# A two-layer GLA/FoX trunk with grouped experts: the residual stays in SBUF through the expert loop, and the router's logits are taken from uncentred rows

## The reference

```python
h = layer_norm(ALPHA * h + mix, ln_g[layer, 0], ln_b[layer, 0])
ffn = grouped_moe(h, router_w, router_bias, moe_w_gate[layer], moe_w_up[layer], moe_w_down[layer])
h = layer_norm(ALPHA * h + ffn, ln_g[layer, 1], ln_b[layer, 1])
# grouped_moe
scores = softmax(xt @ router_w)          # then the best group of 4 experts, and its best 2
h = silu(xt @ w_gate[e]) * (xt @ w_up[e]) * gate[e]
y = sum over the 2 chosen experts of h @ w_down[e]
```

## Time and profile before

| | |
|---|---|
| median of 3 runs | 1231.17 us |
| the profiled execution's own time | 1230.52 us |
| its span | 1228.8 us |
| TensorE busy | 1193.8 us (97%) |
| VectorE busy | 893.2 us (73%) |
| ScalarE busy | 703.7 us (57%) |
| GpSimd busy | 183.9 us (15%) |
| DMA, mean | 229 GB/s |
| weight loads of the experts, each | 1 MB, 12 to 13 us from issue to landing |

### The profile page before, as it was taken

One profiled execution on the slowest core, in us unless ns is written; L12 is line 12 of the kernel. 1 busy time (PEld: TensorE's weight loads), 2 busy tenths in 40 slices (PEclk: granted clock), 3 DMA queues, 4 the chain that ended last, 5 costly groups with the idle time before them and its releaser, 6 DMA issues.

```text
span 1228.8 us, 14990 instructions
## 1 busy us (share of the span) xinstructions
PE 1193.8 (97%) x5802; PEld 945.0 (77%) x5803; DVE 893.2 (73%) x1159; ACT 703.7 (57%) x866; POOL 183.9 (15%) x158
## 2 busy tenths in 40 slices
PE   7999999999999999999999999999999999999995
PEld 5787588877888888876887766768878888888873
DVE  5275555678999998989433555675679999998886
ACT  4432523357687786774333554573267778777672
POOL 1000100211132221210000000000212222122111
PEclk9999999999999999999899999999999999999998
DMA  8223021179999999987111420322289999999973
GB/s 286 71 85 122 1 103 70 52 257 411 358 368 378 368 370 377 358 340 281 69 70 52 154 86 18 103 84 88 78 314 381 373 362 376 379 367 371 370 276 137
DMA packets 66346, 281.52 MB, mean 229 GB/s; under 512 B 12854, under 2 KB 13110, under 8 KB 41698
## 3 DMA queue, kind: packets, MB, share of 16 engines
q1 hardware_dynamic: 49248, 247.55, 53.2%
q0 software_dynamic: 12288, 28.42, 8.1%
q10 hardware_dynamic: 4738, 4.57, 1.1%
HBM read 270.99 MB, written 25.20 MB: 241 GB/s over the span
## 4 chain that ended last, share of the span: by engine, by line
PE 83%; DMA 7%; DVE 6%; issue 2%; ACT 1%; POOL 0%; DVEq 0%; SPq 0%; ACTq 0%; POOLq 0%
PE ps L717 22%; PE ps L719 22%; PE ps L718 22%; DMA ring<-in_moe_w_up_dram 4%; PE ps L885 2%; PE ps L1168 2%; PE ps L1178 2%; DVE ring_r L1613 2%; PE ps L1191 2%; DMA ring<-in_moe_w_down_dram 1%; PE ps L894 1%; DMA ring<-in_kv_w_dram 1%; PE ps L822 1%; PE ps L1099 1%; PE ps L1087 1%
## 5 line engine op out<-in xcount | busy, mean ns | idle before, releaser
L1613 DVE TENSOR_TENSOR ring_r<-ring,ring_r 128x2048 fp32r<-128x2048 f32 x128 | 291.7, 2284 | 7.8 <-ACT ring_r L1346 7.8
L1346 ACT CAST ring_r<-ring 128x2048 fp32r<-128x2048 f32 x128 | 242.6, 1927 | 15.7 <-DMA ring<-in_moe_w_gate_dram 9.8
L718 PE MATMUL ps<-ring_r,xgT_r 128*128 128x512 f32 x528 | 205.9, 390 | 0.0
L1346 ACT CAST high_r<-ring 128x2048 fp32r<-128x2048 f32 x64 | 122.2, 1913 | 113.4 <-DMA ring<-in_moe_w_up_dram 113.4
L1613 DVE TENSOR_TENSOR ring_r<-ring,high_r 128x2048 fp32r<-128x2048 f32 x64 | 146.1, 2289 | 36.3 <-ACT high_r L1346 35.9
L613 POOL DMA_INDIRECT sum_rows<-arena,tokv x28 | 57.7, 2062 | 389.6 <-ACT arena L1399 389.6
L718 PEld LDWEIGHTS ps<-ring_r,xgT_r 128*128 128x128 f32 x528 | 99.3, 188 | 18.8
L717 PE MATMUL ps<-ring_r,xgT_r 128*128 128x512 f32 x272 | 109.1, 401 | 0.2 <-DVE ring_r L1613 0.2
L719 PE MATMUL ps<-ring_r,xgT_r 128*128 128x512 f32 x272 | 106.1, 390 | 0.0
L717 PE MATMUL ps<-high_r,xgT_r 128*128 128x512 f32 x256 | 102.9, 402 | 1.2 <-DVE xgT_r L1827 1.1
L717 PE MATMUL ps<-featT,ring_r 128*128 128x512 f32 x256 | 103.8, 405 | 0.0
(11 more groups left out here) (288 smaller groups left out, 2118.8 us busy)
## 6 DMA issues: line engine op xcount, KB each, us to landing
ring<-in_moe_w_gate_dram SPq DMA_DIRECT2D x64, 1024.0 KB, 12.2
ring<-in_moe_w_up_dram SPq DMA_DIRECT2D x64, 1024.0 KB, 13.0
ring<-in_moe_w_down_dram SPq DMA_DIRECT2D x64, 1024.0 KB, 12.4
ring<-in_gla_w_in_dram SPq DMA_DIRECT2D x6, 2048.0 KB, 9.8
ring<-in_kv_w_dram SPq DMA_DIRECT2D x4, 2048.0 KB, 12.8
ring<-in_fox_w_qg_dram SPq DMA_DIRECT2D x4, 2048.0 KB, 8.1
ring<-in_gla_w_out_dram SPq DMA_DIRECT2D x2, 2048.0 KB, 7.8
h_rows<-arena POOLq DMA_DIRECT2D x8, 512.0 KB, 2.9
```

The source lines that it names most:

```text
L718: pe.matmul(o, left[0], right[1], start=False, stop=False)
L1346: act.copy(high, w).then_inc(half_high, 1)
L1613: dve.tensor_tensor(low, w, high.bitcast(F32), ALU.subtract).then_inc(half_low, 1)
```

## The change

1. The router's weights are multiplied by the gains ahead of time, one copy per layer. For this the gains are loaded as 16 rows of 128 by two small DMAs behind piece 5, TensorE turns them ahead of unit 12, and VectorE makes `g*W` and its column sums.
2. TensorE turns each half tile as soon as VectorE has taken it out of PSUM, in the middle of the next unit. The logits are made in halves too. VectorE's centring now waits until the rows have been turned. The mean times the column sums is subtracted from the logits.
3. The scaling of the last tile is cut in two strided halves, one ahead of the logits' arrival and one behind the difference that ScalarE's exponential waits for.
4. The residual stays in `H`. `sum_rows` becomes one DRAM tensor per layer, filled with zeros by two DMAs that ScalarE issues after unit 15. At the end of a loop the sums are loaded into another place (`moe_sums`), and GpSimd adds each tile to `H`.
5. Two waits are new: `load_sums` waits for the last up-projection, and GpSimd's second-norm work comes behind its four additions.

```diff
# SyncE
                     if n == 3:
                         sp.dma_start(shift_w, ...)
...
+                    if n == 5:
+                        for L in range(DEPTH):
+                            sp.dma_start(gain_rows[L * K:(L + 1) * K, :], ln_g[L, 0:1, :].rearrange("a (k p) -> (a k) p", p=P)
+                                         ).then_inc(shift_loaded, 16)
             def load_sums(L):
...
+                sp.wait_ge(half_used, half_count(L, half_of("up", E - 1, 1)))
                 for t in range(T):
-                    sp.dma_start(H[:, t, :], sum_rows[t * P:(t + 1) * P, :]).then_inc(sums_loaded[t], 16)
+                    sp.dma_start(moe_sums[:, t, :], sum_rows[L][t * P:(t + 1) * P, :]).then_inc(sums_loaded[t], 16)
# GpSimd, start and end of experts
+            const(pool.memset(zeros, 0.0))
...
+                pool.wait_ge(h_ready, T * (2 * L + 1))
+                for t in range(T):
+                    pool.wait_ge(sums_loaded[t], 16 * (L + 1))
+                    pool.tensor_tensor(H[:, t, :], H[:, t, :], moe_sums[:, t, :], ALU.add).then_inc(h_ready, 1)
# TensorE
+LOGITS_AFTER = ({m: (m - 1,) for m in range(1, 2 * T)}, {1: (0,), 3: (2, 1), 4: (3,), 5: (4,), 6: (5,), 7: (6,)})
+            def out_unit(L, u0, m):
+                unit(u0 + m, ks=range(K // 2))
+                if m:
+                    turn_rows_half(L, u0, m - 1)
+                unit(u0 + m, frees=2 if m == 2 * T - 1 else 0, ks=range(K // 2, K))
+                for n in LOGITS_AFTER[L].get(m, ()):
+                    logits_half(L, u0, n)
             def entry_end(L):
                 pe.wait_ge(half_high, half_count(L, 0))
                 idle_products(4, 7)
-                turn_centred(L, T - 1)
+                turn_rows_half(L, OUT_UNITS[L], 2 * T - 1)
                 idle_products(2, 7)
-                logits(L, T - 1)
+                logits_half(L, OUT_UNITS[L], 2 * T - 1)
+            def turn_rows_half(L, u0, m):
+                kk, t = units[u0 + m][2]
+                pe.wait_ge(*taken(u0 + m))
...
+                if m >= 2:
+                    pe.wait_ge(rows_taken, 2 * T * L + m - 1)
+                for j in range(4):
+                    mm = pe.transpose(ps[:, m % 2, j * P:(j + 1) * P],
+                                      H[:, t, (4 * kk + j) * P:(4 * kk + j + 1) * P], ident[:, :])
+                mm.then_inc(rows_turned, 1)
             for u in range(2 * H_A, U_GLA_TAIL):
+                if u == U_GLA_TAIL - 4:
+                    pe.wait_ge(shift_loaded, 16 * (2 * DEPTH + 1))
...
+                    pe.transpose(ps[:, 6, P:P + DEPTH * K], gain_rows, ident[0:DEPTH * K, 0:DEPTH * K]
+                                 ).then_inc(shift_done, 1)
# ScalarE
             take(U_GLA_TAIL - 1)
+            act.wait_ge(consts, 18)
+            for L in range(DEPTH):
+                act.dma_start(sum_rows[L].rearrange("(p r) (c n) -> p (r c) n", p=P, n=P),
+                              zeros.unsqueeze(1).to_broadcast([P, T * K, P])).then_inc(sums_clear, 16)
...
-                for t in range(T):
-                    act.wait_ge(h_scaled, T * L + t + 1)
-                    act.dma_start(sum_rows[t * P:(t + 1) * P, :], H[:, t, :]).then_inc(sums_begun, 16)
# VectorE, rows_normed and router
+                        dve.wait_ge(rows_turned, turned_halves(L, t))
                         dve.scalar_tensor_tensor(out=H[:, t, :], in0=H[:, t, :], scalar=ln_mv[:, t, 0:1], ...
-                scale(N, T - 1)
...
+                do(dve.tensor_tensor(rt[9], over_e(ln_mv[:, :, 0]), each_t(shift_logits[:, DEPTH + L, :], E), ALU.mult))
+                dve.wait_ge(rows_centred, T * L + T)
+                scale_last(2 * L, 0)
                 dve.wait_ge(rt_logits, L + 1)
-                do(dve.tensor_tensor(logits, ps[...], over_e(ln_r[:, :, 1]), ALU.mult))
+                do(dve.tensor_tensor(logits, ps[...], rt[9], ALU.subtract))
+                do(dve.tensor_tensor(logits, logits, over_e(ln_r[:, :, 1]), ALU.mult))
                 do(dve.tensor_tensor(logits, logits, each_t(shift_logits[:, L, :], E), ALU.add))
                 do(dve.tensor_reduce(rv[0], logits, AX.X, ALU.max))
                 dve.tensor_tensor(rt[0], logits, over_e(rv[0]), ALU.subtract).then_inc(rt_in, 1)
+                scale_last(2 * L, 1)
                 dve.wait_ge(rt_exp, L + 1)
# VectorE, second norm: add_first, add_sums
-                    dve.wait_ge(sums_loaded[t], 16 * (L + 1))
+                    dve.wait_ge(h_ready, T * (2 * L + 1) + t + 1)
```

More of the change, by code:

```diff
@@ L74, in yoco_trunk @@
     cum_rows = nc.dram_tensor("cum_rows", [16, S], F32).ap()
-    sum_rows = nc.dram_tensor("sum_rows", [S, D], F32).ap()
+    sum_rows = [nc.dram_tensor(f"sum_rows{L}", [S, D], F32).ap() for L in range(DEPTH)]
     RING, PAIRED = 6, 5
@@ L370, in yoco_trunk, with turned_halves @@
             plan("ob", fox0 + 8 + p, (p, t), "dve")
+        OUT_UNITS = (U_GLA_TAIL + 8, U_OUT)
+        LOGITS_AFTER = ({m: (m - 1,) for m in range(1, 2 * T)}, {1: (0,), 3: (2, 1), 4: (3,), 5: (4,), 6: (5,), 7: (6,)})
+        def turned_halves(L, t, kk=None):
+            at_m = [m for m in range(2 * T) if units[OUT_UNITS[L] + m][2][1] == t and kk in (None, units[OUT_UNITS[L] + m][2][0])]
+            return 2 * T * L + at_m[-1] + 1
         def unit_of(kind, blk):
@@ L609, in gather, with scatter @@
                                         bounds_check=last_row, oob_is_err=False).then_inc(done, 16)
-            def scatter(src, rows, done):
+            def scatter(L, src, rows, done):
                 pool.sem_inc(moves, 1)
-                pool.indirect_dma_start(out=sum_rows, out_offset=bass.IndirectOffsetOnAxis(ap=rows, axis=0),
+                pool.indirect_dma_start(out=sum_rows[L], out_offset=bass.IndirectOffsetOnAxis(ap=rows, axis=0),
                                         in_=src, in_offset=None, bounds_check=last_row, oob_is_err=False,
@@ L657, in experts @@
                                 pool.wait_ge(c_yd, c + 1)
[L658 removed]
+                                scatter(L, cyb, cold_rows[:, 1:2], c_sca)
                             pool.wait_ge(c_sca, (before + 3) * 16)
@@ L783, in tail @@
                         transpose_tile(TP_MIX[L], s - 1, src)
[L785 to L793 removed]
+                for m in range(2 * T):
+                    if m % 2 == 0:
+                        pe.wait_ge(tp_dve, 2 * (4 * TP_MIX[L] + m // 2 + 1))
+                    out_unit(L, u0 + 8, m)
+                entry_end(L)
+            def out_unit(L, u0, m):
[5 more added lines that the diff above has]
+                    logits_half(L, u0, n)
             def idle_products(n, bank):
@@ L1113, in _ @@
                     pe.wait_ge(z_abs, T)
-                    pe.matmul(ps[:, 6, 0:DEPTH * E], one[:, :].to_broadcast([P, P]),
+                    pe.matmul(ps[:, 6, 0:2 * DEPTH * E], one[:, :].to_broadcast([P, P]),
                               shift_sum.rearrange("p a e -> p (a e)"), start=True, stop=True).then_inc(shift_done, 1)
@@ L1209, in _ @@
             for m in range(8):
-                unit(U_OUT + m, frees=2 if m == 7 else 0)
-                if m in (3, 4, 6):
-                    turn_centred(1, (3, 4, 6).index(m))
-                if m in (5, 6, 7):
-                    logits(1, m - 5)
+                out_unit(1, U_OUT, m)
             entry_end(1)
@@ L1290, in take_normed @@
             def take_normed(L):
-                for t in range(T):
-                    for kk in range(2):
-                        act.wait_ge(centred_turned, 2 * (T * L + t) + kk + 1)
-                        act.copy(turned[:, 4 * kk:4 * kk + 4, t * P:(t + 1) * P],
-                                 ps[:, kk, :].rearrange("p (k n) -> p k n", k=4)).then_inc(centred_taken, 1)
-                    if t < T - 1:
-                        scale_residual(L, t)
+                for m in range(2 * T):
+                    kk, t = units[OUT_UNITS[L] + m][2]
+                    act.wait_ge(rows_turned, 2 * T * L + m + 1)
+                    act.copy(turned[:, 4 * kk:4 * kk + 4, t * P:(t + 1) * P],
+                             ps[:, m % 2, :].rearrange("p (k n) -> p k n", k=4)).then_inc(rows_taken, 1)
+                    if L == 0 and kk == 0 and t:
+                        scale_residual(L, t - 1)
+                    if L == 1 and m in (3, 4, 6):
+                        scale_residual(L, (3, 4, 6).index(m))
             def scale_residual(L, t):
                 act.wait_ge(ln_ready, 2 * L * T + t + 1)
-                act.mul(dealt(H[:, t, :], K), blocks(Hp[:, t, :], K), ALPHA).then_inc(h_scaled, 1)
+                act.mul(dealt(H[:, t, :], K), blocks(Hp[:, t, :], K), ALPHA).then_inc(h_ready, 1)
             def tail(L):
@@ L1667, in rows_normed, with scale_last @@
                         done.append(t)
-                dve.wait_ge(rows_centred, T * L + T)
-                scale(N, T - 1)
+            def scale_last(N, part):
+                c, t = slice(part * P // 2, (part + 1) * P // 2), T - 1
```

(10 more changed lines are left out.)

85 lines of the change are left out of this document (39 added, 46 removed).

## The result

The changed kernel takes 1280.26 us (median of 4 runs, 1277.98 to 1280.32), beside 1232.49 us for the kernel before in the same comparison: ratio 1.0377, 95% interval 1.0336 to 1.0418. The forecast was 1252 us, range 1238 to 1267. The sign was right and the size was not: +48 us and not +21. The profiled execution has a span of 1276.2 us beside 1228.8, so there are 47.4 us to find.

The account below looks back on a forecast made before the run. The prediction took TensorE (97% busy) to bound the kernel, with DMA also full in the expert loops. Its terms summed to +21.1 us on the profiled 1230.5 us, plus 0.65 us to the median: 1252 us, range 1238 to 1267.

Parts of the forecast that it names:

- gains: Ahead of unit 12: TensorE waits for the gains' load behind piece 5, +7.7 us, and +1.5 us for its clock.
- zeros: At the heads: issuing the fills holds ScalarE, so TensorE's third output waits, +9.7 us, and +1.0 us for the clock.
- out stages: Both out stages: more half turns and half logits before the last unit ends, 2.1 us each, +4.2 us in all.
- the fifth block: Second layer's out stage: VectorE takes this block late and TensorE wants it in the next unit, +0.5 us.
- the chain behind them: From the last unit's end to the operation behind the exponential: 7.7 us against 7.8 before, counted as 0.
- loops: Expert loops: without storing the residual, TensorE gets back 2 us of idle time per layer, -4.0 us in all.
- GpSimd's additions: Layer ends: four additions of 1.9 us each may delay GpSimd's first norm step; +0.5 us first layer, 0 second.
- Rival B: Expert loops: DMA bounds them and the saved traffic returns in full, 2 x 5.7 us; 1228.4 us, chance 0.06.
- Rivals A and C: A: ScalarE not held by the fills, 1241.6 us, chance 0.22; C: slower fills, clock down through heads, 1267.5 us, chance 0.12.

Follow-up runs that it names:

- the router part alone: Kernel before with logits from uncentred rows, gains loaded behind piece 3 and 29 idle products, residual still through DRAM: 1240.2 us (ratio 1.0069).
- the two kernels of the residual part: Kernel before with the residual kept in SBUF and zero fills by SyncE: 1235.58 us with additions by VectorE, 1228.65 us with additions by DMA.
- the kernel with early gains: Changed kernel with the gains loaded behind piece 3 and not behind piece 5: 1270.5 us (ratio 1.0301).

## Why the prediction came out too low

From the marks, the terms measured against the forecast are (us): gains 10.4 (9.2 with the clock), zeros 7.4 (10.7), out stages 5.5 (4.7 with the fifth block), the chain behind them -0.5 (0), picked experts to gates 8.1 (0), gates to the first hidden blocks 0.8 (0), loops -1.8 (-4.0), last hidden block to first sum 15.4 (0.5), first norm to out stage 2 2.2 (0). Of the 26 us that were missing, 15 are the additions and 8 the tables, both put at about nothing.

- **Gains, +7.7 and +1.5 for the clock: right.** 8.34 us of standstill (8.4 forecast) and about 2.3 us of half clock (twelve matmuls at 0.2 us more each); undone, 9.8 us.
- **Zeros, +9.7 and +1.0: that the issue holds ScalarE is right, the rule for its end is not, and the size was too large.** ScalarE was held 12.5 us and not 17.2. The prediction had it held until only 2500 pieces were open; 4968 packets had still not begun. The prices were good: a piece of 512 B took 27.2 ns (30 forecast) and piece 6 stood in the way for 6.3 us per DMA engine (6.5 forecast), by the row below. Only 3256 packets of the fills came first, 5.5 us per engine and not 10.7. Undone, 9.2 us; between the changed kernel's marks 7.4 us (17.72 at the end of the heads less 10.35 at unit 15).

DMA queues of the changed kernel from 110 to 136.61 us, where the issue ended (packets, MB, share of 16 engines; q1 is SyncE's with piece 6, q10 ScalarE's with the fills):

```profile
q1 hardware_dynamic: 1040, 2.10, 23.7%
q10 hardware_dynamic: 3256, 1.67, 20.8%
```

- **Out stages, +4.2: nearly right**, 2.7 and 2.8 us and not 2.1 each. The +0.5 us for the fifth block shows only as the 0.1 between the two.
- **"The logits come early, but VectorE isn't free for them ... I count 0": the chain right, the conclusion wrong.** From the last eviction to the operation behind the exponential it is 7.5 us (7.7 forecast). But TensorE's 20 idle products begin with the early logits. They ended 2.0 us before the picked experts came, the clock fell, and the tables took 3.7 and 4.4 us more. With 29 idle products this went. The step that failed is asking only whether VectorE gains by early logits, and not what TensorE does in the time. The later second half of the scaling, some 2 us at the gather, lay hidden under it.
- **GpSimd's additions, +0.5 and 0: the step that failed most.** I sized them by their own length (1.9 us forecast, at most 2.8; 2.3 us beside the one-hots and 3.3 beside the splits) and asked who waits for them. Nobody waited for them; VectorE's work beside them was kept out. It cost 5.9 us in the first layer, and in the second 9.4 us with the clock. The prediction took it, without a word, that GpSimd and VectorE work side by side at no cost to each other; with that fall both the +0.5 and "in the second layer ... I count nothing". That the second layer pays at all hangs on the sums' landing, 2 us earlier or later.
- **Loops, -4.0: too much.** 1.1 and 0.7 us came back from the first hidden block to the last, and the router part alone gives as much with no traffic saved. In the other kernels it goes from 2.1 us back to 0.8 us lost. With the start of the loop unmoved, as in the two kernels of the residual part, 0.8 to 1.4 us come back; more than that the saved traffic is not shown to be worth. Rival B, all of it back, is out.
- Rivals A and C are out: ScalarE was held, for less time than my own term. The total came near C's for reasons that C doesn't name.

What stays open: why the clock falls in some profiles and not in others behind the same gap, and what ends a long issue. The narrow matmuls behind the second norm show what such a difference is worth. From the first sum to the first eviction of out stage 2 the kernel with early gains took 3.4 us more than the changed one, though nothing differs there. Its clock in the three stretches of 10 us around those matmuls was 0.87, 0.50 and 0.95, and the changed kernel's 1.00, 0.66 and 1.00. That is the 1.2 GHz level for some 14 and some 7 us, 3.4 us of work (an estimate): the whole difference. So of the sums above the terms from marks are firmer than those from totals.

## What to carry to other kernels

Work given to GpSimd is not only its own length: list what VectorE does in the same microseconds with two SBUF inputs or in SBUF-to-SBUF scalar form, and count for each addition one such operation that is held, here by 1.5 to 2.2 us. When a step on TensorE comes earlier, look at the filler behind it that was counted for the old gap. And before an engine is given an addition, see whether the DMA that brings the operand can make it: here that was 7 us quicker than VectorE's additions, of which some 2 us are clock.

## What the runs showed of the hardware

- GpSimd's float32 addition of 128x1024 takes 2.33 us beside VectorE's one-hots and 3.3 us beside its subtractions; VectorE does it in 1.22 us. One-hots that collide with it come singly between additions, at 2.4 us each.
- Two issues, of 8192 pieces of 512 B together, hold the issuing engine's queue 12.5 us (12.1 on SyncE), two of 4096 of 1 KB together 9.3 us; the first of the two takes 0.6 us. 4968 and 3481 packets had not begun when the second ended.
- Adding DMAs from DRAM onto SBUF: four of 512 KB, issued in 3.7 us, landed after 12.2 us (median) beside weight pieces of 2 MB; plain loads took 6.2 to 8.7 us.
